# A last head normed by thirds, and attention's weights one slot ahead, in a one-core encoder step on Trainium2

## What is computed

```python
def _gla_block(q, k, v, la, s):
    b = jnp.cumsum(la, axis=1)
    qd, kd = q * jnp.exp(b), k * jnp.exp(-b)
    a = jnp.where(tril, jnp.einsum('blhk,bshk->bhls', qd, kd), 0.0)
    o = jnp.einsum('blhk,bhkv->blhv', qd, s) + jnp.einsum('bhls,bshv->blhv', a, v)
    s_new = s * jnp.exp(b[:, -1])[..., None] + jnp.einsum(
        'bshk,bshv->bhkv', k * jnp.exp(b[:, -1][:, None] - b), v)
    return o, s_new
...
    o = o * lax.rsqrt(jnp.mean(o * o, axis=-1, keepdims=True) + EPS)
    o = o * norm_g.astype(jnp.float32).reshape(GLA_HEADS, GLA_DV)
    return (o * jax.nn.silu(g)) @ w_out, s_fin
...
def _attend(q, k, v, bias, valid):
    s = jnp.einsum('bqhd,bkhd->bhqk', q, k) * (ATT_DH ** -0.5) + bias[None]
    s = jnp.where(valid, s, NEG_INF)
    p = jax.nn.softmax(s, axis=-1)
    return jnp.einsum('bhqk,bkhd->bqhd', p.astype(v.dtype), v)
```

## Time and profile before

| | us |
|---|---|
| median of three runs | 2986.18 (2981.93 to 2991.45) |
| the profiled execution, its own time | 2985.14 |
| its span, first to last instruction | 2983.2 |
| PE busy | 2836.3 (95%) |
| DVE / ACT / POOL busy | 1326.0 / 1017.3 / 1009.1 |
| mean granted TensorE clock | 0.975 |

### The profile page before, as it was taken

One profiled execution on the slowest core, in us unless ns is written; L12 is line 12 of the kernel. 1 busy time (PEld: TensorE's weight loads), 2 busy tenths in 40 slices (PEclk: granted clock), 3 DMA queues, 4 the chain that ended last, 5 costly groups with the idle time before them and its releaser, 6 DMA issues. The chain is left out here.

```text
span 2983.2 us, 49668 instructions
## 1 busy us (share of the span) xinstructions
PE 2836.3 (95%) x19878; PEld 2655.1 (89%) x19878; DVE 1326.0 (44%) x2443; ACT 1017.3 (34%) x1968; POOL 1009.1 (34%) x694
## 2 busy tenths in 40 slices
PE   7999997989999999999899999997989999999999
PEld 5888885989999999999778788865989999999998
DVE  5233333586565553111433333343685565552122
ACT  4434433442232233110444434344432222223123
POOL 2121221644444447331311212102744444456420
PEclk8999998999999999999899999999999999999998
DMA  5222212722222216220423333336422222235211
GB/s 180 72 79 73 64 56 81 232 82 87 73 67 82 74 60 236 80 68 17 153 86 99 113 99 113 93 94 204 143 91 85 67 71 85 68 107 197 91 43 64
DMA packets 341955, 292.89 MB, mean 98 GB/s; under 512 B 25008, under 2 KB 307648, under 8 KB 341216
## 3 DMA queue, kind: packets, MB, share of 16 engines
q1 hardware_dynamic: 341728, 289.73, 30.7%
HBM read 220.67 MB, written 91.01 MB: 104 GB/s over the span
## 5 line engine op out<-in xcount | busy, mean ns | idle before, releaser
L83 PE MATMUL f_ps<-f_x_hi,f_w_hi 128*128 128x288 f32 (+3 forms) x2904 | 904.0, 311 | 22.9 <-POOL f_x_lo L749 10.1
L84 PE MATMUL f_ps<-f_x_hi,f_w_lo 128*128 128x288 f32 (+3 forms) x2904 | 900.6, 310 | 0.0
L85 PE MATMUL f_ps<-f_x_lo,f_w_hi 128*128 128x288 f32 (+3 forms) x2904 | 898.8, 309 | 0.0
L83 PEld LDWEIGHTS f_ps<-f_x_hi,f_w_hi 128*128 128x128 f32 x2904 | 548.6, 189 | 27.5 <-DVE f_x_lo L1119 11.8
L85 PEld LDWEIGHTS f_ps<-f_x_lo,f_w_hi 128*128 128x128 f32 x2904 | 550.4, 190 | 1.9
L84 PEld LDWEIGHTS f_ps<-f_x_hi,f_w_lo 128*128 128x128 f32 x2904 | 549.2, 189 | 2.0
L736 POOL TENSOR_TENSOR f_w_lo<-f_w_whole,f_w_hi 128x512 fp32r<-128x512 f32 x136 | 192.0, 1420 | 391.2 <-DVE f_w_whole L1153 171.8
L1306 DVE TENSOR_TENSOR res<-res,f_ps 128x384 f32<-128x384 f32 (+2 forms) x192 | 106.3, 554 | 434.0 <-PE f_ps L85 424.8
L1176 DVE TENSOR_TENSOR res<-f_ps,res 128x288 f32<-128x288 f32 x308 | 140.1, 457 | 209.1 <-PE f_ps L85 199.9
L1176 DVE TENSOR_TENSOR f<-f_ps,f 128x288 f32<-128x288 f32 x308 | 139.7, 457 | 160.4 <-PE f_ps L85 150.1
L83 PE MATMUL f_ps<-f_x_hi 128*128 128x288 f32 (+2 forms) x584 | 180.2, 309 | 25.4 <-DVE f_x_lo L1188 25.4
(11 more groups left out here) (308 smaller groups left out, 5785.8 us busy)
## 6 DMA issues: line engine op xcount, KB each, us to landing
f_x_whole<-hid_rows SPq DMA_DIRECT2D x44, 576.0 KB, 4.8
f_raw<-in_ffn_w_down SPq DMA_DIRECT2D x48, 384.0 KB, 3.5
hid_rows<-f SPq DMA_DIRECT2D x44, 288.0 KB, 2.1
hid_rows<-res SPq DMA_DIRECT2D x44, 288.0 KB, 2.1
mix_w_stage<-in_gla_w_in SPq DMA_DIRECT2D x24, 512.0 KB, 3.7
f_raw<-in_ffn_w_gate SPq DMA_DIRECT2D x22, 512.0 KB, 4.0
f_raw<-in_ffn_w_up SPq DMA_DIRECT2D x22, 512.0 KB, 5.3
res<-in_ffn_w_gate SPq DMA_DIRECT2D x22, 512.0 KB, 4.0
```

Of the source, the lines that this page charges most:

```text
L83: pe.matmul(out, w_hi, x_hi, start=first, stop=False)
L84: pe.matmul(out, w_lo, x_hi, start=False, stop=False)
L85: return pe.matmul(out, w_hi, x_lo, start=False, stop=last)
```

## The change

In the recurrence's last head the root, the reciprocal and the gating are made in three parts: tiles 0 to 2 in slot 4, tiles 3 to 5 in slot 7, tiles 6 to 8 behind slot 8. The turnings of tiles 0 to 5 go into the slots 4 to 8 (`OWN`), those of the tiles 6, 7 and 8 behind the stream updates 3, 4 and 5 (`WITH_STREAM`). The streams' updates stand behind the slot's projection now. The last streams' states leave in two stores of four streams.

In attention each weight is fetched one slot earlier and the units are dealt one to a slot; POOL splits before it masks and spreads. `SOON[3]` is rounded in slot 1 of the loop. The projections of the pairs 4, 5 and 6 are dealt one to a slot, and three tiles of values move to pair 6, whose outputs now wait tile by tile for their values. `load_bias_s` issues 16 DMAs instead of 24.

```diff
+    OWN = {4: (0,), 5: (1,), 6: (2,), 7: (3,), 8: (4, 5)}
+    OWN_NORM = {4: 0, 7: 1}
+    AT_END = range(2 * NG, NT)
...
+        if h == H - 1:
+            out += [("o", h * NT + n) for n in OWN.get(i, ())]
...
+            WITH_STREAM = {n: i for n, i in zip((3, 4, 5), AT_END)}
...
-                send_states(H - 1)
-                for i in range(NT):
+                sp.wait_ge(stepped, (H - 1) * (NB + DEC_B) + NB)
+                sp.dma_start(a["state_gla_prompt"][0, 0, H - 1, :, :], st_fin[:]).then_inc(st_out, 16)
+                send_streams(H - 1, slice(0, DEC_B // 2))
+                for i in AT_END[:2]:
                     send_mixed((H - 1) * NT + i)
+                send_streams(H - 1, slice(DEC_B // 2, DEC_B))
+                send_mixed(SLOTS - 1)
...
-                for i in range(NT):
-                    fill(("o", (H - 1) * NT + i))
+                for n in range(DEC_B):
+                    update_stream(H - 1, n)
+                    if n in WITH_STREAM:
+                        fill(("o", (H - 1) * NT + WITH_STREAM[n]))
...
                     if i == 0 and h:
-                        root(h - 1)
+                        root(h - 1, slice(0, NT))
+                    if h == H - 1 and i in OWN_NORM:
+                        root(h, slice(OWN_NORM[i] * NG, (OWN_NORM[i] + 1) * NG))
...
                     keep_out(s)
+                    if h == H - 1 and i in OWN_NORM:
+                        for n in range(NG):
+                            gate_out(h * NT + OWN_NORM[i] * NG + n)
                     if i == SAMPLE:
                         for n in range(DEC_B):
                             step_stream(h, n)
+                            if h == H - 1 and n in WITH_STREAM:
+                                gate_out(h * NT + WITH_STREAM[n])
...
-        if p % 2 == 0:
+        if p == PAIRS - 4:
+            plan = ["k0", "k1", "k2", "v0", "q0", "v1", "q1", "v2", "q2"]
+        elif p == PAIRS - 3:
+            plan = ["k0", "v3", "k1", "q0", "k2", "v4", "q1", "v5", "q2"]
+        elif p == PAIRS - 2:
+            plan = ["k0", "v6", "k1", "q0", "v7", "k2", "v8", "q1", "q2"]
+            m = p // 2
+        elif p % 2 == 0:
             plan = ["k0", "k1", "k2", "v0", "q0", "v1", "q1", "v2", "q2v3"]
         else:
             plan = ["k0v4", "k1", "k2v5", "q0", "v6", "q1", "v7", "q2", "v8"]
...
-        if p % 2 == 0 and j == 0 and 0 < p < PAIRS - 2:
-            out += [("v", p // 2 + 1, c) for c in range(2)]
-        if 0 < p < PAIRS - 1 and j == 1:
-            out.append(("q", p + 1, 0))
+        if p % 2 == 0 and j < 2 and 0 < p < PAIRS - 2:
+            return [("v", p // 2 + 1, j)]
+        if 0 < p < PAIRS - 1 and j == (1 if p % 2 else 2):
+            return [("q", p + 1, 0)]
         if p < PAIRS - 2 and j == 4:
-            out.append(("k", p + 2, 0))
-        return out
+            return [("k", p + 2, 0)]
...
-                        for x in units_of(s):
+                        for x in units_of(s + 1):
                             fetch(x)
...
+                    for x in units_of(s):
+                        scale_and_split(x)
                     if j == 2:
                         if p:
                             mask_sample(p)
                         spread_queries(p)
-                    for x in units_of(s):
-                        scale_and_split(x)
...
-                for x in SOON[2:]:
-                    round_weights(x)
+                round_weights(SOON[2])
...
                         for x in units_of(s):
                             round_weights(x)
+                        if s == 1:
+                            round_weights(SOON[3])
```

More of the change, by code:

```diff
@@ L1395, in fills_of @@
             out += [("o", (h - 1) * NT + NG * i + n) for n in range(NG)]
+        if h == H - 1:
+            out += [("o", h * NT + n) for n in OWN.get(i, ())]
         return out + [("l", n) for n in third_of(s, 0)]
     FILLS = [("l", t) for t in range(NG)] + [("k", 0)] + [x for s in range(SLOTS) for x in fills_of(s)] + \
-        [("o", (H - 1) * NT + i) for i in range(NT)]
+        [("o", (H - 1) * NT + i) for i in AT_END]
     FILL = {x: n for n, x in enumerate(FILLS)}
@@ L1541, in send_states, with send_streams @@
                     sp.dma_start(a["state_gla_prompt"][0, 0, h, :, :], st_fin[:]).then_inc(st_out, 16)
-                    sp.dma_start(a["state_gla_sample"][0, :, h, :, :].rearrange("b k v -> k b v"), st_s[:]).then_inc(st_out, 16)
+                    send_streams(h, slice(0, DEC_B))
+                def send_streams(h, part):
+                    sp.wait_ge(stepped, h * (NB + DEC_B) + NB + part.stop)
+                    sp.dma_start(a["state_gla_sample"][0, part, h, :, :].rearrange("b k v -> k b v"), st_s[:, part]
+                                 ).then_inc(st_out, 16)
                 def send_mixed(n):
@@ L1781, in _ @@
                     out(s)
-                    if i == SAMPLE:
+                    if i == SAMPLE and h < H - 1:
                         for n in range(DEC_B):
@@ L1826, in square, with root @@
                     act.activation(sq[:], o[:, i, :], ACT.Square, accum_out=ss[:, i:i + 1]).then_inc(squared, 1)
-                def root(h):
-                    act.wait_ge(squared, (h + 1) * NT)
+                def root(h, part):
+                    act.wait_ge(squared, h * NT + part.stop)
                     if h:
                         act.wait_ge(gated, h * NT)
-                    act.activation(rms[:], ss[:], ACT.Sqrt, bias=S.eps[:], scale=1.0 / VW).then_inc(rooted, 1)
+                    act.activation(rms[:, part], ss[:, part], ACT.Sqrt, bias=S.eps[:], scale=1.0 / VW).then_inc(rooted, 1)
                 def take(x):
@@ L1925, in _ @@
                         grow(n)
-                root(H - 1)
-                for i in range(NT):
+                root(H - 1, slice(2 * NG, NT))
+                for i in AT_END:
                     take(("o", (H - 1) * NT + i))
@@ L2039, in gate_out @@
                     h, i = at_slot(n)
-                    if i == 0:
-                        dve.wait_ge(rooted, h + 1)
-                        dve.reciprocal(rms[:], rms[:]).then_inc(inverse, 1)
-                        dve.wait_ge(inverse, h + 1)
-                        dve.wait_ge(done["g"], COUNT["g", h, NT - 1])
+                    last_head = h == H - 1
+                    if i % NG == 0 if last_head else i == 0:
+                        part = slice(i, i + NG if last_head else NT)
+                        dve.wait_ge(rooted, norms_before(h, i))
+                        dve.reciprocal(rms[:, part], rms[:, part]).then_inc(inverse, 1)
+                        dve.wait_ge(inverse, norms_before(h, i))
+                        dve.wait_ge(done["g"], COUNT["g", h, part.stop - 1])
                     if n >= 3:
@@ L2086, in _ @@
                             take_kq(x)
-                for i in range(NT):
-                    gate_out((H - 1) * NT + i)
 def attention(nc, S, a, tag):
@@ L2150, in units_of @@
         p, j = tile_of(s)
-        out = []
-        if p % 2 == 0 and j == 0 and 0 < p < PAIRS - 2:
-            out += [("v", p // 2 + 1, c) for c in range(2)]
-        if 0 < p < PAIRS - 1 and j == 1:
-            out.append(("q", p + 1, 0))
+        if p % 2 == 0 and j < 2 and 0 < p < PAIRS - 2:
+            return [("v", p // 2 + 1, j)]
+        if 0 < p < PAIRS - 1 and j == (1 if p % 2 else 2):
+            return [("q", p + 1, 0)]
         if p < PAIRS - 2 and j == 4:
-            out.append(("k", p + 2, 0))
-        return out
+            return [("k", p + 2, 0)]
+        return []
     EARLY = [("k", 0, 0), ("q", 0, 0), ("v", 0, 0), ("v", 0, 1)]
@@ L2297, in load_bias_s @@
                             new = S.strips[2 * p + h, 0, ZERO:ZERO + 1]
-                            for g in range(2):
-                                sp.dma_start(bias_s[rows, g, :PAST], bass.AP(
-                                    tensor=past.tensor, offset=past.offset, ap=[[STRIP - 1, DEC_S], [1, PAST]])
-                                ).then_inc(bias_s_in, 16)
+                            sp.dma_start(bias_s[rows, :, :PAST], bass.AP(
+                                tensor=past.tensor, offset=past.offset, ap=[[STRIP - 1, DEC_S], [0, 2], [1, PAST]])
+                            ).then_inc(bias_s_in, 16)
                             sp.dma_start(own[rows, :], bass.AP(
@@ L2373, in _ @@
                             load_keys(p, 1)
-                        if j == 3 and p % 2 == 0:
+                        if p % 2 == 0 and j == (SAMPLE if p == PAIRS - 2 else 3):
                             send_values(p // 2)
@@ L2554, in out @@
                     vb, vf = p // 2 % 2, p % 2 * P
-                    if j == 0 and p % 2 == 0:
+                    if p == PAIRS - 2:
+                        pe.wait_ge(v_done, BY_SCALAR["v", p // 2, j] + 1)
+                    elif j == 0 and p % 2 == 0:
                         pe.wait_ge(v_done, BY_SCALAR["v", p // 2, NT - 1] + 1)
```

6 lines of the change are left out of this document (4 added, 2 removed).

## The result

| us | before | after |
|---|---|---|
| median of five runs on one chip | 2984.23 (2980.86 to 2991.45) | 2959.15 (2952.44 to 2961.64) |
| ratio after to before | | 0.9907 (0.9887 to 0.9928) |
| the profiled execution, its own time | 2985.14 | 2952.44 |
| its span | 2983.2 | 2950.5 |

The changed kernel is 25.1 us faster by the medians. The forecast was 2955, with a range of 2946 to 2968, so the time lies in the range, 4 us above the forecast. Between the two profiled executions the gain is 32.7 us. That is more than the medians show, since the profiled execution of after is the fastest of its five, 6.7 us under its median, and that of before lies 0.9 over.

What follows compares the result with a forecast made beforehand. PE, busy 95% of the span, bounds the kernel; only its pauses and low-clock time can be won. Terms 15.1 + 5.4 + 6.1 + 0.5 + 3.4 = 30.5 off 2985.1 give 2954.6, said as 2955; range 2946 to 2968.

Steps and rivals of the forecast that it cites:

- The fetch one slot ahead: Attention, slot 5 of pairs 0 to 5: PE's waits for ACT's output copy and three clock drops go, 15.1 us.
- the 0.6 kept as a remainder: Slot 5 of six pairs: 0.1 us of pause a pair left standing, subtracted from the 11.3 us of waits.
- slot 5 stays late: Rival, chance 0.22: ACT's rounding leaves 0.7 us pauses in six pairs, drops in half; 8.7 us come back, 2964.
- The weights come no earlier: Rival, chance 0.08: a slot's stores hold SP, so the earlier place in its list fetches no sooner; about 2973 us.
- Value halves in two slots: Attention, slot 1 of pairs 2 and 4: two pauses of 1.96 and a drop of 1.45 go, 5.4 us.
- `SOON[3]`: Attention, slot 1 of pair 0: a pause of 4.24 and a clock drop taken as 1.9 go, 6.1 us.
- all goes: Slot 1 of pair 0: the whole pause of 4.24 us disappears, as 5.5 us leave ACT's path.
- Projections dealt anew: Attention, pairs 4 to 6: 3.6 us gained, less a new wait of 2.3 and 0.8 for its drop; net 0.5.
- with a projection in each this goes, 3.6 us: Pair 6's three empty slots: pauses of 0.78, 1.44 and 1.35 us go once each holds a projection.
- The recurrence's last head: End of the recurrence: gating in parts and two state stores bring 3.4 us, between 1.9 and 4.6.
- so 1.95 a turn: Recurrence's end: gating 0.45, turning 0.3, stream update 0.74 and step 0.46 alternate on PE and DVE, 1.95 us each.
- The rule of the drain: Rival, chance 0.02: each ACT table switch costs a drain of about 1.38 us besides its load; 2.8 us back, 2957.

Runs made afterwards that it cites:

- The recurrence's part alone: Kernel before with only the recurrence's edits, attention as before: 2984.16 us, ratio 0.9984 to the kernel before.
- the late fetch: Changed kernel with each weight fetched in the slot of its rounding, as before the change: 2970.72 us, ratio 0.9948 to the kernel before.
- the early query weights: Changed kernel with pair 7's query weight rounded in slot 1 of pair 6 instead of slot 2: 2952.29 us, ratio 0.9879 to the kernel before.
- the old dealing: Changed kernel with the projections of pairs 4, 5 and 6 dealt as before the change: 2952.84 us, ratio 0.9897 to the kernel before.
- the `SOON` edit: Changed kernel with both last `SOON` weight halves rounded ahead of the loop, as before the change: 2958.86 us, ratio 0.9914 to the kernel before.
- its repetition: Changed kernel, unedited, measured once more on another run's chip: 2955.93 us, ratio 0.9909 to the kernel before.
- The gatings in a row: Changed kernel with the last three gatings together behind stream step 3, not behind steps 3, 4 and 5: 2956.31 us, ratio 0.9892 to the kernel before.

## Why the prediction was right, and where it was off

**The fetch one slot ahead: right, place and size.** The six slots 5 took 62.3 us before and 45.3 now. 1.2 of this difference is the new dealing, which put a shorter piece into pair 5's slot (7.14, where pair 3 has 8.34), so 15.8 remain, for the 15.1 of the sum. No pause at all was left, so the 0.6 kept as a remainder was not needed. Of the 15.8, 4.5 are drops of the clock, as many as the trace of before happened to have: three behind six pauses. The recurrence's part alone and the late fetch have three too, partly in other pairs, so the number was no special luck, though which pauses they follow is chance. The rival "slot 5 stays late" gave 2964 and falls: ACT's rounding, hidden by nothing on ACT, still ended in time. "The weights come no earlier" falls by the late fetch, whose trace is what that rival described, and which comes out at 2970.7 where the rival said 2973.

**Value halves in two slots: right.** Slot 1 of pair 2 fell by 10.66 - 7.21 = 3.45, that of pair 4 by 9.21 - 7.21 = 2.00, 5.4 in all as summed.

**`SOON[3]`: right.** The slot fell by 11.49 - 5.78 = 5.7, for 6.1. A pause of 0.48 us stays, so the step "all goes" was wrong by this much. The drop, taken as 1.9 without a twin to compare, was 7.25 less 5.30 of busy time, 1.95; with the edit undone it was 1.5.

**Projections dealt anew: the term was mis-sized, 0.5 for -0.8.** The step "with a projection in each this goes, 3.6 us" held, since the three pauses are gone. The new wait was forecast at 2.3 and measured 1.92. Its drop was charged at 0.8, 1.5 by five chances in nine. It came in five of six traces with the wait, with 1.57 us. So the forecast's two ends, 1.3 without the drop and -0.2 with it, measured 0.9 and -0.8. What the step missed: the new plans put the queries' last group, alone, into slot 8 of the pairs 4 and 5, and PE there waits 0.74 for DVE to take them, as it already did in pair 6 before. With the early query weights 3.1 us of gain stay. The step's own terms give 3.6 - 1.5 = 2.1. The other 1.0 is product time: PE is busy 199.1 us in these three pairs with the old dealing and 198.0 with the new one, both at the full clock. The step took product time as only moved. Why it shrank is not shown.

**The recurrence's last head: right in its order of events, mis-sized in one term.** The delay by table loads and turnings was taken as 0.9. Before, the slots 4 to 7 took 5.69 us each; after, slot 4 took 5.91, slot 5 6.35 and the others 5.69, which makes 0.88. The first gating was forecast at 499.2 in the time of the trace of before; less the 1.3 us by which the trace of after runs ahead there, 497.9, and it began at 497.89. From there to the issue of the last states' store 6.5 us were forecast and 8.14 were measured (506.03). The step that failed is "so 1.95 a turn". It was right at the full clock: in the traces of the early query weights, the `SOON` edit and the old dealing the two turns took 1.84 or 1.85 each. But it added durations at the full clock, and in after, its repetition, the recurrence's part alone and the late fetch the clock fell inside the chain, with turns of 2.06 to 2.51. Where it held until the last turn, the stage from the last head to the SwiGLU took 79.3 to 79.5 us, a gain of 2.6 to 2.8; where it fell, 80.5 to 81.6. The store landed in 2.9, for 3.0 (issue line and tiles, KB each, median us to landing):

```profile
out_state_gla_sample<-mix_state_sample SPq DMA_DIRECT2D x2, 512.0 KB, 2.9
```

From its landing to the SwiGLU's first product it was 10.6 us, where before has 10.5 behind its last store. So 3.4 less 1.6 for the chain and 0.2 for the restart is the 1.6 of the table. The gatings in a row confirm the term from the other side: with no turns to wait for, the store is 4.1 us sooner.

**The rule of the drain.** In the rows above the load at 488.41 lasts 1.28 and the gate begins at 489.71, 0.02 after its end; the second new load cost slot 7 nothing. In after, 46 of 51 loads have their activation within 0.02 us of their end; the activations of the other five wait for PE or DVE. The other runs have the same five, so no drain of 1.38 us shows in any. The Trainium skill (ScalarE: Activation LUTs, What ACT_TABLE_LOAD costs) states one; here the measurement decides against it, and the 2.8 us of that rival did not come.

**The total.** By place the change gave 15.8 + 5.4 + 5.7 - 0.8 + 1.6 = 27.7, for 30.5 forecast. The recurrence's end fell short by 1.8 and the dealing by 1.3, `SOON[3]` by 0.4; the fetch gave 0.7 more. The 26.1 of attention is itself known to some 3 us only, by chance drops: the same attention code took 560.7 and 564.0 before, and 534.6, 537.4 and 536.2 after, which gives 23.3 to 29.4. The sum lies between the two measures of the whole, 25.1 by the medians and 32.7 by the profiled spans; the interval of the ratio is 21 to 34 us and holds both. Most of the 5.0 by which the spans go beyond the sum is not the change. The second SwiGLU, the same code in all kernels, took 915.1 us to its last product in the trace of before and 910.1 in that of after. Its windows, first 887.6 us and then the rest, before:

```profile
2062.40:2950.00 887.60, 875.62 (x5970) 861.60 (x5971) 440.44 (x685) 270.54 (x433) 397.44 (x237) 0.99 0.31 99
2950.00:2977.50 27.50, 26.53 (x178) 26.05 (x177) 8.40 (x21) 8.41 (x21) 0.00 (x0) 0.75 0.16 62
```

and after:

```profile
2034.10:2921.70 887.60, 875.74 (x5956) 862.11 (x5957) 443.82 (x684) 269.87 (x431) 398.29 (x237) 0.99 0.31 99
2921.70:2944.30 22.60, 21.60 (x192) 21.07 (x191) 9.23 (x22) 9.36 (x22) 0.00 (x0) 1.00 0.20 79
```

The first part is the same to 0.1 us of PE's time; the end lasts 4.9 us longer before, at PEclk 0.75. The prediction allowed 4.5 us for chance drops and took them to follow pauses. This one follows none, and the allowance had no term for it. The remaining terms, POOL's new order and the 16 bias loads, were forecast at nothing and no run takes them alone; in the pairs 0 to 3 no slot but 1 and 5 differs by more than 0.04 us between the two traces.

## What to carry to other kernels

When the busiest engine waits for a copy, read what the copying engine did just before: here it stood behind a cast that waited for a weight, and one slot of lead for the fetch took six such waits and the clock drops behind them away, about 15 us here. When work is dealt evenly over slots, look again at the slot that each weight and each result now meets: the evened plan brought next to nothing until its weight came a slot earlier. A chain that alternates between two engines costs a turn for every step. The short steps of one engine in a row were 2.8 us cheaper here at the full clock. The clock fell inside the chain of turns in four traces of seven, and in one of three with the gatings in a row, so that turns bring the drop is not shown.

## What the runs showed that was not expected

The low clock can come with no pause of PE ahead of it. The second SwiGLU took 910.0 to 912.9 us in nine traces, 915.1 and 915.6 in those of before and of the early query weights, and 922.4 in that of the `SOON` edit, whose end reads

```profile
2924.30:2959.10 34.80, 33.83 (x197) 33.20 (x195) 9.51 (x22) 9.36 (x22) 0.00 (x0) 0.66 0.15 61
```

with PE busy 33.83 of 34.80 us at PEclk 0.66, behind 887.6 us at 0.99. It set in 892 to 894 us into the stage in each of the five traces that have it, and lasted between 6.8 and 23.9 us; a 128x128 product took 0.42 us in it, and 0.27 before. What PE did just before is the same in all: at 886 to 888 us its products change from 128x512 to smaller ones of 128x128, with no pause between 870 us and the drop. The other seven traces have this change too, and no drop. So why it comes in one execution and not in another is open; no run tried to bring it about.

A pause of about 2 us is sometimes followed by a stretch at 1.2 GHz that costs 1.3 to 1.6 us, and sometimes not: the wait of 1.92 us at slot 3 of pair 6 was followed by it in five traces and not in the sixth, the same pause of the same code. Pair 7 pauses 0.8 to 1.6 us in each of its slots 1 to 7, in every trace, and had no short drop in five traces, one in four, two in two and three in one. This alone moves attention's time by 1.5 to 4.7 us.
